# Retention, attention and a three-branch block: the order of the steps inside the attention groups, and where an output product starts

## The chip, the cores and the metric

The kernel runs on one core of a Trainium2 chip. The metric is the device time in microseconds (us) of one execution, as the median of several; lower is better. TensorE (PE) multiplies, ScalarE (ACT) and VectorE (DVE) do the element-wise work, SyncE (SP) issues most of the DMAs, GpSimd (POOL) is hardly used. Each engine runs its own list of instructions in order, and they meet through semaphores.

## The reference, cut to what matters

The input is one sequence of 256 tokens of width 2048, a context of 256 tokens and a memory of 256 tokens, all in float32. Two layers come first: a retention layer (8 heads) and an attention layer. Then comes a block with three attention branches. The change lies mostly in the attention layer:

```python
q = rms_norm(heads(h_lat @ w_in[q]), q_gain)      # 16 heads of 128
k = rms_norm(heads(h @ w_in[k]), k_gain)          # 4 kv heads; latent and context tokens
v = heads(h @ w_in[v]); g = h_lat @ w_in[g]
q, k = rope_2d(q), rope_2d(k)                     # latent tokens only
p = softmax(concat([q @ k_window, q @ k_ctx, sink]))   # each kv head serves a group of 4 q heads
y = (p @ v * silu(g)) @ w_out
x = x + gate * y
```

The retention layer ends likewise: `(norm(o) * silu(g)) @ w_out`, with `o` 512 wide for each of the 8 heads.

## The kernel before

**Weights.** All weight matrices come as one stream of 936 chunks of 128 x 1024 float32 (STREAM, built by `stream_order`). SP issues one DMA a chunk into one of four `raw` buffers, as soon as DVE is done with the chunk that was there (`sync_program`). A product is made of three in a reduced float32 format: the weights are split into `w_hi` (a copy by ACT, L921) and `w_lo` (the rest, a subtraction by DVE, L1429), the activations likewise into hi and lo, and PE adds hi*hi, hi*lo and lo*hi (`product`, L510 to L512). `w_hi` and `w_lo` have four buffers each too, so ACT may copy chunk n once PE is done with chunk n-4. On ACT and DVE `weights_to(c)` does all splits up to chunk c+3 that are not yet done; `ahead(what)` calls it with the last chunk of a tile. It is called at fixed places of the two programs, so a split waits for whatever stands ahead of it on its engine.

**Tiles and pairs.** `tile` (PE) makes 128 output columns of a product over all 16 k tiles: two chunks, 48 matmuls. `pair` makes 2 x 128 output columns over 4 k tiles (one chunk, 24 matmuls), for the output products: `attn_out(kv)` is 8 pairs, as is `ret_out(h)`. Its result is added to the residual `res` by DVE (`add_out`, L1608).

**Banks.** PSUM has eight banks, and `bank` takes them in turn. PE waits there until the bank's last result was read: `pair` takes both of its banks before its first matmul, a head's scores take two banks, its transposes two, a gate, a next q tile, a value product and `q_means` one each.

**Attention.** After the values (av), the four k tiles (ak) and the q tiles of group 0 (aq) are made. Each k tile is normed: a mean by PE (L708), a root by ACT (L959), a reciprocal, a scaling and a rotation by DVE (`norm`; the rotation waits until ACT has swapped halves of the tile, L992 and L993). Then four groups follow, one for each kv head. A step of a head is: `z` gate tile (PE), tanh (ACT, L986) and its product with the gate (DVE, L1497); `sc` scores (PE, L719), a masked read out of PSUM, maximum and so on (DVE, L1776 to L1788), exp (ACT, L1185), scaling to probabilities `a_s` (DVE, L1796); `tr` transposes (PE, L729), copied by ACT into `a_pt` (L1192); `pv` the value product (PE, L738), gated by DVE (L1803), whose hi part is a copy by ACT (`a_o_hi`, L1197) and whose lo part is DVE's (`a_o_lo`, L1806). The q tiles of the next group are made between them, their squares summed by `q_means` (L748), with a root by ACT and a reciprocal by DVE. The order of group kv on PE is

```
z0 z1 sc0 z2 sc1 tr0 z3 pv0 sc2 nq0 tr1 sc3 nq1 pv1 tr2 nq2 pv2 tr3 nq3 pv3 [o_lo(3)] attn_out(kv)
```

with nq the next group's q tiles (none in group 3) and `q_means` of the next group inside attn_out. ACT and DVE have lists in the same order. After group 3 DVE adds squares of the result (L1447), PE makes their mean x2 (L592), and the next block's input can be made (L1883).

## Time and profile before

| | us |
|---|---|
| median of three runs | 3464.83 |
| lowest and highest | 3459.5, 3465.22 |
| the profiled execution | 3462.32 |
| its span, first to last instruction | 3461.0 |
| PE busy in it | 3266.4 |
| DVE, ACT busy | 1710.4, 1260.8 |

The profile page gives each engine's busy time over the span and the chain of work that ended last. The trace behind it can be asked for the instructions of a stretch in order of time, for the waits of one engine, and for the busy time and the TensorE clock that was granted (1.00 is the full one) in any stretch. Times in the trace count from the span's start. Of the layers, retention ends at about 1863 us, the attention groups run from 2015 to 2368 us, and the last block takes the rest.

### The profile page before, as it was taken

The page shows a single profiled execution, that of the slowest core. Times are in us where ns is not written, and L with a number is a line of the kernel's source. Part 1 is how long each engine was busy: PE and PEld are TensorE (multiplying, and loading weights), DVE is VectorE, ACT ScalarE, POOL GpSimd, SP SyncE. Part 2 cuts the span into 40 slices and gives each one's busy share as a digit, 9 for nine tenths or more (in the row PEclk, how much of TensorE's full clock was granted, in tenths as well). Part 3 has the DMA queues.
Part 4 walks back from the last instruction along what each step waited for, and adds up shares of the span by engine and source line. Part 5 has one row for each costly group of instructions (what it writes and reads, how often), then busy time and mean ns, then how long its engine had stood idle before and what let it go on. Part 6 is the DMA issues. An engine that isn't in the chain of part 4 may idle for free.

```text
span 3461.0 us, 47818 instructions
## 1 busy us (share of the span) xinstructions
PE 3266.4 (94%) x20346; PEld 2791.9 (81%) x20346; DVE 1710.4 (49%) x2479; ACT 1260.8 (36%) x1785; POOL 0.2 (0%) x4
## 2 busy tenths in 40 slices
PE   6879999999999999999997989988999999999998
PEld 5657677777777777777766889987999999999998
DVE  5433343434333343443336566766665555555555
ACT  4342222222222222222224455544554444444443
POOL 0000000000000000000000000000000000000000
PEclk9989999999999999999998999999999999999999
DMA  7744423233332333333233234433445444455554
GB/s 304 289 187 158 179 107 110 104 128 122 110 128 95 113 109 128 122 110 128 86 142 138 86 122 146 138 131 137 162 149 168 149 158 161 156 190 199 193 188 153
DMA packets 141635, 508.93 MB, mean 147 GB/s; under 512 B 15344, under 2 KB 19568, under 8 KB 140656
## 3 DMA queue, kind: packets, MB, share of 16 engines
q1 hardware_dynamic: 137040, 493.03, 40.5%
q10 hardware_dynamic: 4384, 12.85, 1.0%
q8 instruction: 161, 2.64, 0.3%
q14 instruction: 50, 0.41, 0.0%
HBM read 501.62 MB, written 4.19 MB: 146 GB/s over the span
## 4 chain that ended last, share of the span: by engine, by line
PE 88%; DVE 4%; DMA 3%; ACT 3%; issue 2%; SPq 0%; ACTq 0%; DVEq 0%
PE bank L510 26%; PE bank L512 26%; PE bank L511 26%; DMA raw<-stream 3%; PE bank L563 2%; PE bank L653 2%; PE bank L719 1%; PE bank L738 1%; DVE w_lo L1429 1%; PE bank L639 1%; PE bank L655 1%; PE bank L729 1%; ACT a_s L1185 0%; ACT w_hi L921 0%; PE bank L579 0%
## 5 line engine op out<-in xcount | busy, mean ns | idle before, releaser
L510 PE MATMUL bank<-h_hi,w_hi 128*128 128x256 f32 (+1 forms) x4032 | 1268.1, 315 | 16.1 <-DVE w_lo L1429 13.8
L1429 DVE TENSOR_TENSOR w_lo<-raw,w_hi 128x1024 fp32r<-128x1024 f32 x744 | 901.4, 1223 | 757.4 <-ACT w_hi L921 753.3
L511 PE MATMUL bank<-h_lo,w_hi 128*128 128x256 f32 (+1 forms) x4032 | 1245.8, 309 | 0.0
L512 PE MATMUL bank<-h_hi,w_lo 128*128 128x256 f32 (+1 forms) x4032 | 1245.6, 309 | 0.0
L921 ACT ACTIVATE w_hi<-raw 128x1024 fp32r<-128x1024 f32 x744 | 780.3, 1057 | 1073.2 <-PE bank L512 608.1
L510 PEld LDWEIGHTS bank<-h_hi,w_hi 128*128 128x128 f32 x4032 | 762.5, 189 | 84.7 <-issue 34.0
L511 PEld LDWEIGHTS bank<-h_lo,w_hi 128*128 128x128 f32 x4032 | 764.0, 189 | 45.3 <-issue 3.3
L512 PEld LDWEIGHTS bank<-h_hi,w_lo 128*128 128x128 f32 x4032 | 762.0, 189 | 43.7
L510 PE MATMUL bank<-w_hi,h_hi 128*128 128x512 f32 x704 | 292.6, 416 | 47.8 <-DVE h_lo L1481 20.6
L511 PE MATMUL bank<-w_lo,h_hi 128*128 128x512 f32 x704 | 281.7, 400 | 0.0
L512 PE MATMUL bank<-w_hi,h_lo 128*128 128x512 f32 x704 | 281.4, 400 | 0.0
L1608 DVE SCALAR_TENSOR_TENSOR res<-bank,mod,res 128x256 f32<-128x256 f32 x320 | 134.2, 478 | 177.7 <-PE bank L512 177.6
L510 PE MATMUL bank<-o_hi,w_hi 128*128 128x512 f32 x512 | 201.2, 393 | 12.5 <-ACT vg L981 9.8
L510 PEld LDWEIGHTS bank<-w_hi,h_hi 128*128 128x128 f32 x704 | 136.7, 194 | 94.3 <-issue 40.2
L511 PE MATMUL bank<-o_lo,w_hi 128*128 128x512 f32 x512 | 200.2, 391 | 0.0
L512 PE MATMUL bank<-o_hi,w_lo 128*128 128x512 f32 x512 | 200.2, 391 | 0.0
L512 PEld LDWEIGHTS bank<-w_hi,h_lo 128*128 128x128 f32 x704 | 136.2, 193 | 30.7
L511 PEld LDWEIGHTS bank<-w_lo,h_hi 128*128 128x128 f32 x704 | 136.7, 194 | 29.6 <-issue 1.9
L563 PE MATMUL bank<-raw,cond 128*32 128x256 f32 x1536 | 115.7, 401 | 19.3 <-DMA raw<-stream 19.3
L510 PEld LDWEIGHTS bank<-o_hi,w_hi 128*128 128x128 f32 x512 | 96.7, 189 | 34.8 <-issue 15.0
L512 PEld LDWEIGHTS bank<-o_hi,w_lo 128*128 128x128 f32 x512 | 96.6, 189 | 20.3
L511 PEld LDWEIGHTS bank<-o_lo,w_hi 128*128 128x128 f32 x512 | 96.7, 189 | 19.8
(219 smaller groups left out, 2667.1 us busy)
## 6 DMA issues: line engine op xcount, KB each, us to landing
raw<-stream SPq DMA_DIRECT2D x936, 512.0 KB, 4.0
res<-tokens_in ACTq DMA_DIRECT2D x4, 1024.0 KB, 7.5
vg<-mem_in ACTq DMA_DIRECT2D x4, 512.0 KB, 8.9
res<-mem_kv ACTq DMA_DIRECT2D x2, 1024.0 KB, 9.4
out<-res SPq DMA_DIRECT2D x4, 512.0 KB, 3.0
mem_kv<-qk ACTq DMA_DIRECT2D x1, 1024.0 KB, 12.6
mem_kv<-vg ACTq DMA_DIRECT2D x1, 1024.0 KB, 15.8
tab<-tables ACTq DMA_DIRECT2D x1, 512.0 KB, 4.8
```

Of the source, the lines that this page charges most:

```text
L510: pe.matmul(out, sh, mh, start=start, stop=False)
L511: pe.matmul(out, sh, ml, start=False, stop=False)
L512: return pe.matmul(out, sl, mh, start=False, stop=stop)
L563: mm = pe.matmul(out[32 * j:32 * j + 32, 0:L], m.cond[:, 4 * c + j, :], m.raw[SLOT[chunk]][:, j * L:(j + 1) * L], start=c == 0, stop=c == 3)
L639: mm = pe.matmul(outs[mt][:, :], m.qk[:, 2 + dt, L + mt * P:L + (mt + 1) * P], m.qk[:, dt, :], start=dt == 0, stop=dt == 1)
L653: pe.matmul(out[:, :], m.v[:, 2 + mt, dv], m.s_ctx[:, mt, :], start=mt == 0, stop=mt == 1)
L655: mm = pe.matmul(out[:, LAT], m.v[:, mt, dv], m.s_lat[:, mt, :], start=False, stop=mt == 1, skip_group_check=True)
L719: mm = pe.matmul(out[:, at - a0:at - a0 + n], q[:, qs], k, start=i == 0, stop=i == len(pairs) - 1)
L729: mm = pe.transpose(out[:, at:at + P], probs[:, qt, kt * P:(kt + 1) * P], ident)
L921: act.activation(m.w_hi[n % SLOTS][:, :], m.raw[SLOT[raw]][:, :], ACT.Copy).then_inc(s.hi, 1)
L1429: dve.tensor_tensor(m.w_lo[slot][:, :], m.raw[SLOT[raw]][:, :], m.w_hi[slot][:, :].bitcast(F32), ALU.subtract).then_inc(s.lo, 1)
L1608: i = dve.scalar_tensor_tensor(out=m.res[:, tile, cols], in0=psum(*what)[:, cols], scalar=m.mod[layer][:, 2 * KT + tile, side:side + 1], i ...
```

## The change

1. `pair` can be given four semaphore values (`ready`), one for each k tile. Then it loops k outside and output j inside, and waits for tile k's value ahead of its products. The first pair of every `ret_out` and `attn_out` uses it, in place of one wait for `o_lo` of the last tile ahead of the product.
2. The k norms on ACT and DVE call `weights_to` between the root or scaling and the swap or rotation.
3. Gate tile 0 of the next group and `q_means` of the next group are made at the end of a group, ahead of `attn_out`; the groups 1 to 3 begin with z1.
4. `attn_out(2)` moves into group 3, behind sc1. On ACT and DVE its pairs 0 to 2 stand ahead of sc(1), the other five behind it.
5. In group 3, z2 and z3 stand behind sc2 and sc3.

The stream of chunks is put into the same order. Per group and engine no instruction is added or taken away.

```diff
@@ -182,14 +182,26 @@
         tile(("ak", i), "attn_w_in", q_w + i * P)
     for h in range(GROUP):
         tile(("aq", 0, h), "attn_w_in", h * P)
-    for i in range(ATTN_KV):
-        for h in range(GROUP):
+
+    def az(i, *heads):
+        for h in heads:
             tile(("az", i, h), "attn_w_in", q_w + 2 * kv_w + (GROUP * i + h) * P)
-        if i < ATTN_KV - 1:
-            for h in range(GROUP):
-                tile(("aq", i + 1, h), "attn_w_in", (GROUP * (i + 1) + h) * P)
+
+    def attn_out(i):
         for n in range(KT // 2):
             out.append((("attn_out", i), "attn_w_out", 0, 4 * i, 4, n * 2 * P, 2 * P))
+    az(0, 0)
+    for i in range(ATTN_KV - 1):
+        az(i, 1, 2, 3)
+        for h in range(GROUP):
+            tile(("aq", i + 1, h), "attn_w_in", (GROUP * (i + 1) + h) * P)
+        az(i + 1, 0)
+        if i < ATTN_KV - 2:
+            attn_out(i)
+    az(ATTN_KV - 1, 1)
+    attn_out(ATTN_KV - 2)
+    az(ATTN_KV - 1, 2, 3)
+    attn_out(ATTN_KV - 1)
     for n in range(2):
         for c in range(8):
             values(("bv", n), "w_in_2", 2 * W_A + n * 512, c)
@@ -525,16 +537,17 @@
                              k == 0, k == k_tiles - 1)
             mm.then_inc(s.mm, 1)
 
-    def pair(what, c, cols, acts, k0=0):
+    def pair(what, c, cols, acts, k0=0, ready=None):
 
         xh, xl = acts
         outs = [bank(*what, j) for j in range(2)]
         wh, wl = weights(c)
-        for j in range(2):
-            for k in range(4):
-                w = slice(k * 2 * P + j * P, k * 2 * P + (j + 1) * P)
-                mm = product(outs[j][:, 0:cols.stop - cols.start], (wh[:, w], wl[:, w]),
-                             (xh[:, k0 + k, cols], xl[:, k0 + k, cols]), k == 0, k == 3)
+        for j, k in [(j, k) for k in range(4) for j in range(2)] if ready else [(j, k) for j in range(2) for k in range(4)]:
+            if ready and j == 0:
+                pe.wait_ge(*ready[k])
+            w = slice(k * 2 * P + j * P, k * 2 * P + (j + 1) * P)
+            mm = product(outs[j][:, 0:cols.stop - cols.start], (wh[:, w], wl[:, w]),
+                         (xh[:, k0 + k, cols], xl[:, k0 + k, cols]), k == 0, k == 3)
         mm.then_inc(s.mm, 1)
 
     def values_banks(what, tiles):
@@ -686,9 +699,9 @@
             beside(h, "end")
             ada(1, 21)
             ada_turn(1, 20)
-        pe.wait_ge(*s["o_lo"].at(h, 3))
         for n in range(KT // 2):
-            pair(("ret_out", h, n), FIRST["ret_out", h] + n, BOTH, (m.o_hi, m.o_lo))
+            pair(("ret_out", h, n), FIRST["ret_out", h] + n, BOTH, (m.o_hi, m.o_lo),
+                 ready=[s["o_lo"].at(h, k) for k in range(4)] if n == 0 else None)
     ada_turn(1, 21)
     ada(1, 22)
     mean("x1", BOTH)
@@ -775,36 +788,57 @@
         def next_q(h):
             if not last:
                 tile(("aq", kv + 1, h), LAT)
-        z(0)
+        def attn_out(kv):
+            for n in range(KT // 2):
+                pair(("attn_out", kv, n), FIRST["attn_out", kv] + n, LAT, (m.a_o_hi, m.a_o_lo),
+                     ready=[s["o_lo"].at("a", kv, k) for k in range(4)] if n == 0 else None)
         if kv == 0:
+            z(0)
             q_means(0)
         z(1)
         pe.wait_ge(*s["roped"].at("aq", kv, 1))
         pe.wait_ge(*s["roped"].at("ak", ATTN_KV - 1))
         sc(0)
-        z(2)
-        sc(1)
-        tr(0)
-        z(3)
-        pe.wait_ge(*s["v_set"].at("a", kv))
-        pv(0)
-        sc(2)
-        next_q(0)
-        tr(1)
-        sc(3)
-        next_q(1)
-        pv(1)
-        tr(2)
-        next_q(2)
-        pv(2)
-        tr(3)
-        next_q(3)
-        pv(3)
-        pe.wait_ge(*s["o_lo"].at("a", kv, 3))
-        for n in range(KT // 2):
-            if n == 2 and not last:
-                q_means(kv + 1)
-            pair(("attn_out", kv, n), FIRST["attn_out", kv] + n, LAT, (m.a_o_hi, m.a_o_lo))
+        if not last:
+            z(2)
+            sc(1)
+            tr(0)
+            z(3)
+            pe.wait_ge(*s["v_set"].at("a", kv))
+            pv(0)
+            sc(2)
+            next_q(0)
+            tr(1)
+            sc(3)
+            next_q(1)
+            pv(1)
+            tr(2)
+            next_q(2)
+            pv(2)
+            tr(3)
+            next_q(3)
+            pv(3)
+            tile(("az", kv + 1, 0), LAT)
+            q_means(kv + 1)
+            if kv < ATTN_KV - 2:
+                attn_out(kv)
+        else:
+            sc(1)
+            attn_out(kv - 1)
+            tr(0)
+            pe.wait_ge(*s["v_set"].at("a", kv))
+            pv(0)
+            sc(2)
+            z(2)
+            tr(1)
+            pv(1)
+            sc(3)
+            z(3)
+            tr(2)
+            pv(2)
+            tr(3)
+            pv(3)
+            attn_out(kv)
     mean("x2", LAT)
 
 
@@ -1148,11 +1182,12 @@
         act.wait_ge(*source)
         act.activation(m.nsq[i][:, :], x, ACT.Square).then_inc(*s["squared"].up(*what))
 
-    def norm(what, i, x, before):
+    def norm(what, i, x, before, after):
 
         if before:
             act.wait_ge(*s["roped"].at(*before))
         root(("norm", *what), s["n_meaned"].at(*what), m.nrstd[i][:, :])
+        weights_to(FIRST[after])
         n = x.shape[1]
         swap(what, m.nrstd[i][:, 0:n * L].rearrange("p (a b) -> p a b", b=L), x, 32, s["n_scaled"].at(*what))
 
@@ -1201,11 +1236,12 @@
     for n in range(1, ATTN_KV):
         ahead(("ak", n))
         norm_squares(("ak", n), n % 2, m.a_k[:, n, :], banks.at("ak", n))
-        norm(("ak", n - 1), (n - 1) % 2, m.a_k[:, n - 1:n, LAT], ("ak", n - 3) if n >= 3 else None)
+        norm(("ak", n - 1), (n - 1) % 2, m.a_k[:, n - 1:n, LAT], ("ak", n - 3) if n >= 3 else None,
+             ("ak", n + 1) if n < ATTN_KV - 1 else ("aq", 0, 0))
     ahead(("aq", 0, 0))
     q_square(0, 0)
     n = ATTN_KV - 1
-    norm(("ak", n), n % 2, m.a_k[:, n:n + 1, LAT], ("ak", n - 2))
+    norm(("ak", n), n % 2, m.a_k[:, n:n + 1, LAT], ("ak", n - 2), ("aq", 0, 1))
     ahead(("aq", 0, 1))
     q_square(0, 1)
     q_swap(0, 0, ("ak", 2))
@@ -1240,39 +1276,60 @@
         def next_swap(n):
             if not last:
                 q_swap(kv + 1, n, ("aq", kv, n))
-        z(0)
+        def attn_out(kv, *pairs):
+            for n in pairs:
+                weights_to(FIRST["attn_out", kv] + n)
+                if kv == ATTN_KV - 1:
+                    for j in range(2):
+                        k = 2 * n + j
+                        act.wait_ge(*banks.at("attn_out", kv, n, j))
+                        square("x2", k, (sq_out(k, LAT), m.res[:, k, LAT]))
         if kv == 0:
+            z(0)
             q_root(0)
         z(1)
         sc(0)
-        z(2)
-        sc(1)
-        tr(0)
-        z(3)
-        pv(0)
-        sc(2)
-        next_q(0)
-        tr(1)
-        sc(3)
-        next_q(1)
-        pv(1)
-        tr(2)
-        next_swap(0)
-        next_q(2)
-        pv(2)
-        tr(3)
-        next_q(3)
-        pv(3)
-        next_swap(1)
-        for n in range(KT // 2):
-            weights_to(FIRST["attn_out", kv] + n)
-            if n == 2 and not last:
-                q_root(kv + 1)
-            if last:
-                for j in range(2):
-                    k = 2 * n + j
-                    act.wait_ge(*banks.at("attn_out", kv, n, j))
-                    square("x2", k, (sq_out(k, LAT), m.res[:, k, LAT]))
+        if not last:
+            z(2)
+            sc(1)
+            tr(0)
+            z(3)
+            pv(0)
+            sc(2)
+            next_q(0)
+            tr(1)
+            sc(3)
+            next_q(1)
+            pv(1)
+            tr(2)
+            next_swap(0)
+            next_q(2)
+            pv(2)
+            tr(3)
+            next_q(3)
+            pv(3)
+            next_swap(1)
+            tanh(("az", kv + 1, 0), m.a_g[:, 0, :])
+            q_root(kv + 1)
+            if kv < ATTN_KV - 2:
+                attn_out(kv, *range(8))
+        else:
+            attn_out(kv - 1, 0, 1, 2)
+            sc(1)
+            attn_out(kv - 1, 3, 4, 5, 6, 7)
+            tr(0)
+            pv(0)
+            sc(2)
+            z(2)
+            tr(1)
+            pv(1)
+            sc(3)
+            z(3)
+            tr(2)
+            pv(2)
+            tr(3)
+            pv(3)
+            attn_out(kv, *range(8))
     root(("mean", "x2"), s["meaned"].at("x2"), m.rstd[:, LAT])
 
 
@@ -1730,13 +1787,14 @@
         done(what)
         dve.tensor_copy(x, psum(*what)[:, 0:cols.stop - cols.start]).then_inc(*banks.up(*what))
 
-    def norm(what, i, x, latent, gain):
+    def norm(what, i, x, latent, gain, after):
 
         dve.wait_ge(*banks.at("norm", *what))
         dve.reciprocal(m.nrstd[i][:, :], m.nrstd[i][:, :]).then_inc(*s["n_rstd"].up(*what))
         dve.wait_ge(*s["n_rstd"].at(*what))
         dve.scalar_tensor_tensor(out=x, in0=x, scalar=gain, in1=m.nrstd[i][:, :], op0=ALU.mult, op1=ALU.mult
                                  ).then_inc(*s["n_scaled"].up(*what))
+        weights_to(FIRST[after])
         n = latent.shape[1]
         cos, sin = [m.rope1[:, j, :].unsqueeze(1).broadcast_to([P, n, L]) for j in range(2)]
         rotate(what, latent, m.nrstd[i][:, 0:n * L].rearrange("p (a b) -> p a b", b=L), cos, sin, s["n_scaled"].at(*what))
@@ -1757,8 +1815,8 @@
         dve.wait_ge(*banks.at("q_mean", kv))
         dve.reciprocal(m.q_rstd[:, :, :], m.q_rstd[:, :, :]).then_inc(*s["q_rstd"].up(kv))
 
-    def k_norm(n):
-        norm(("ak", n), n % 2, m.a_k[:, n, :], m.a_k[:, n:n + 1, LAT], m.gains[:, 1:2])
+    def k_norm(n, after):
+        norm(("ak", n), n % 2, m.a_k[:, n, :], m.a_k[:, n:n + 1, LAT], m.gains[:, 1:2], after)
 
     def softmax(what, x, width, numbers, mask, sink, rstd=None):
 
@@ -1808,9 +1866,9 @@
     tile_in(("ak", 0), m.a_k[:, 0, :], BOTH)
     for n in range(1, ATTN_KV):
         tile_in(("ak", n), m.a_k[:, n, :], BOTH)
-        k_norm(n - 1)
+        k_norm(n - 1, ("ak", n + 1) if n < ATTN_KV - 1 else ("aq", 0, 0))
     q_in(0, 0)
-    k_norm(ATTN_KV - 1)
+    k_norm(ATTN_KV - 1, ("aq", 0, 1))
     q_in(0, 1)
     q_rotate(0, 0)
     q_in(0, 2)
@@ -1836,39 +1894,54 @@
             if not last:
                 q_in(kv + 1, h)
 
-        z(0)
+        def attn_out(kv, *pairs):
+            for n in pairs:
+                weights_to(FIRST["attn_out", kv] + n)
+                dve.wait_ge(s.mm, FIRST["attn_out", kv] + n + 1)
+                for j in range(2):
+                    add_out(("attn_out", kv, n, j), 2 * n + j, (0,), 1)
+                if kv == ATTN_KV - 1:
+                    for j in range(2):
+                        add_square("x2", 2 * n + j, LAT)
         if kv == 0:
+            z(0)
             q_reciprocal(0)
         z(1)
         dve.wait_ge(*s["q_rstd"].at(kv))
         sc(0)
-        z(2)
-        sc(1)
-        z(3)
-        pv(0)
-        sc(2)
-        next_q(0)
-        sc(3)
-        next_q(1)
-        pv(1)
         if not last:
+            z(2)
+            sc(1)
+            z(3)
+            pv(0)
+            sc(2)
+            next_q(0)
+            sc(3)
+            next_q(1)
+            pv(1)
             q_rotate(kv + 1, 0)
-        next_q(2)
-        pv(2)
-        next_q(3)
-        pv(3)
-        if not last:
+            next_q(2)
+            pv(2)
+            next_q(3)
+            pv(3)
             q_rotate(kv + 1, 1)
-        for n in range(KT // 2):
-            weights_to(FIRST["attn_out", kv] + n)
-            dve.wait_ge(s.mm, FIRST["attn_out", kv] + n + 1)
-            for j in range(2):
-                add_out(("attn_out", kv, n, j), 2 * n + j, (0,), 1)
-            if n == 2 and not last:
-                q_reciprocal(kv + 1)
-            if last:
-                for j in range(2):
-                    add_square("x2", 2 * n + j, LAT)
+            silu(("az", kv + 1, 0), m.a_g[:, 0, :])
+            q_reciprocal(kv + 1)
+            if kv < ATTN_KV - 2:
+                attn_out(kv, *range(8))
+        else:
+            attn_out(kv - 1, 0, 1, 2)
+            sc(1)
+            attn_out(kv - 1, 3, 4, 5, 6, 7)
+            pv(0)
+            sc(2)
+            z(2)
+            pv(1)
+            sc(3)
+            z(3)
+            pv(2)
+            pv(3)
+            attn_out(kv, *range(8))
     reciprocal(("mean", "x2"), m.rstd[:, LAT], ("x2",))
 
 
```

## Rows read from the trace of the kernel before

**Rows 1.** The page: the span, and one engine's busy time, share and instructions.

```profile
span 3461.0 us, 47818 instructions
PE 3266.4 (94%) x20346; PEld 2791.9 (81%) x20346; DVE 1710.4 (49%) x2479; ACT 1260.8 (36%) x1785; POOL 0.2 (0%) x4
```

**Rows 2.** PE's waits, 1950 to 2430 us: releaser, us in total, times, longest.

```profile
PE bank L510 <- DVE a_o_lo L1806: 8.6, 4, 3.0
PE bank L738 <- ACT a_pt L1192: 8.5, 3, 4.4
PE bank L592 <- DVE sq_sum L1447: 7.2, 1, 7.2
PE bank L510 <- DVE w_lo L1429: 5.6, 2, 5.1
...
PE bank L738 <- issue: 3.8, 4, 1.9
```

**Rows 3.** PE's waits, 250 to 1820 us (the retention heads).

```profile
PE bank L510 <- ACT vg L981: 9.8, 7, 1.5
...
PE bank L510 <- DVE w_lo L1429: 2.7, 1, 2.7
```

**Rows 4.** Stretches on PE: us, busy (instructions), granted clock, DMA share, GB/s.

```profile
2109.20:2120.50 11.30, 11.30 (x98) 1.00 0.54 186
2182.40:2199.40 17.00, 17.00 (x145) 1.00 0.57 196
```

**Rows 5.** Timeline of PE: start, us, instruction, idle before it and releaser.

```profile
2003.83 0.58 PE L510 MATMUL bank<-h_hi,w_hi 128*128 128x256 f32 x1 [5.15 <-DVE w_lo L1429]
...
2265.09 0.38 PE L510 MATMUL bank<-a_o_hi,w_hi 128*128 128x256 f32 x1 [2.98 <-DVE a_o_lo L1806]
...
2346.34 0.38 PE L510 MATMUL bank<-a_o_hi,w_hi 128*128 128x256 f32 x1 [1.42 <-DVE a_o_lo L1806]
```

**Rows 6.** Timeline of DVE in the last k norms and behind them.

```profile
1990.55 0.43 DVE L1488 TENSOR_TENSOR a_k<-a_k,a_rope 128x256 f32<-128x256 f32 x1 [1.83 <-ACT a_rstd L993]
...
2001.43 0.43 DVE L1488 TENSOR_TENSOR a_k<-a_k,a_rope 128x256 f32<-128x256 f32 x1 [1.82 <-ACT a_rstd L993]
...
2010.34 2.35 DVE L1429 TENSOR_TENSOR w_lo<-raw,w_hi 128x1024 fp32r<-128x1024 f32 x2
```

**Rows 7.** Timeline of PE: `q_means`, then a value product, scores and transposes.

```profile
2180.66 1.84 PE L748 MATMUL bank<-a_ones,a_sq 128*128 128x1 f32 x16
...
2318.36 1.97 PE L738 MATMUL bank<-a_pt,a_v 128*128 128x256 f32 x8 [0.64 <-issue]
2320.16 1.88 PE L719 MATMUL bank<-a_k,a_q 128*128 128x512 f32 x4
2321.87 1.04 PE L729 MATMUL bank<-tab,a_s 128*128 128x128 f32 x8
```

**Rows 8.** Timeline of DVE, groups 2 and 3.

```profile
2269.20 1.22 DVE L1429 TENSOR_TENSOR w_lo<-raw,w_hi 128x1024 fp32r<-128x1024 f32 x1
...
2303.47 1.53 DVE L1776 SCALAR_TENSOR_TENSOR a_s<-bank,a_q_rstd,a_mask 128x512 f32<-128x512 f32 x2
...
2309.76 2.35 DVE L1429 TENSOR_TENSOR w_lo<-raw,w_hi 128x1024 fp32r<-128x1024 f32 x2
...
2349.38 0.88 DVE L1608 SCALAR_TENSOR_TENSOR res<-bank,mod,res 128x256 f32<-128x256 f32 x2 [1.35 <-PE bank L512]
```

**Rows 9.** Timeline of ACT, group 3.

```profile
2295.18 1.28 ACT L986 ACT_TABLE_LOAD   x1
...
2317.20 1.05 ACT L1192 ACTIVATE a_pt<-bank 128x512 f32<-128x512 f32 x2
```

**Rows 10.** Stretches on PE behind a wait, columns as in rows 4.

```profile
2003.80:2009.60 5.80, 5.77 (x27) 0.50 0.50 184
2265.10:2267.50 2.40, 2.40 (x13) 0.63 0.67 218
2329.00:2340.90 11.90, 8.88 (x25) 0.65 0.00 0
```

## Prediction

> **What bounds the kernel now.** Read the page's busy shares first: TensorE (PE) is busy 94% of 3461.0 us, VectorE (DVE) 49% [rows 1]. So only what PE stands still for, or runs slowly for, can be won. I then listed PE's waits over the attention part alone, 1950 to 2430 us, where nearly the whole diff acts: 8.6 us for a_o_lo in four waits (one ahead of each group's output product), 8.5 us for a_pt in three (all in group 3), 7.2 us for the last square sum, 5.6 us for w_lo in two (while the q tiles of group 0 are made), 3.8 us marked "issue" ahead of value products [rows 2]. That is 34 us, besides what the slower clock costs behind the longer gaps. Group 3 is the weak place: it has no next q tiles to lay between its heads.
>
> **Output products begin with the k tiles that are there.** Twelve first pairs (8 ret_out, 4 attn_out) get four waits in place of one, and their 24 products go k outside, j inside. In the heads PE's waits at these places are for ACT's copies of the values out of PSUM (L981: 9.8 us, seven times), which free the banks that the pair takes before its first product, and once 2.7 us for w_lo, the pair's own weights [rows 3]. Neither goes: both must be there before k tile 0 too. Gain in ret_out: 0. The extra waits are on semaphores long raised; a boundary between two attn_out pairs, which has three such waits, doesn't show in a stretch of 145 product rows that took 17.00 us (0.117 each) [rows 4]. Cost taken: 0; at the most 0.1 us at each of 36, 3.6 us.
>
> **Weights inside the k norms.** Before, PE waited 5.15 us at 2003.83 for the second half of aq2's weights, since DVE copied none between its two norms [rows 5]. DVE stood 1.83 and 1.82 us in these norms until ACT's swap was done [rows 6]. The change puts one w_lo (1.15 of a row of two at 2.35) into each of these holes, so DVE's own chain moves up by about 1.13 us twice, 2.3 us. PE's chain: aq1 without its 0.47 us wait; aq2's second half at about 1998 (2003.83 less 5.15 and 0.47), w_lo there at 1999.7 (2001.43 less the hole of 1.82, less 1.13, plus 1.2): 2 us of waiting left; aq3's first half to 2005.5; its second needs the row that began at 2010.34 [rows 6], now 2008.1 plus 1.15, so PE waits 3.8 us there, where before its late and slow start had hidden that. The stall mostly moves. What counts is DVE's chain into the first softmax, since PE waited behind it too (the longest "issue" wait, 1.9 us, is at group 0's first pv) [rows 2]. It comes 2.3 us earlier; the clock behind the 3.8 us gap may make PE the late one by some 0.6. Taken: 1.7 us. Bounds: 0.4, if PE runs slowly through aq3 and z0, and 2.3; 8.2 if all the 5.6 us of waiting and the slow clock behind it went (27 product rows in 5.80 us [rows 10], 2.6 more than at 0.117), which the 2010.34 row speaks against.
>
> **Groups 0 and 1.** The next group's gate tile 0 (5.65 us: 98 rows in 11.30 us are two tiles) [rows 4] and q_means (1.7 us) [rows 7] now stand between pv(3) and attn_out. o_lo is ready at most 3.0 us behind pv(3), so their two waits go (8.6 less 2.98 and 1.42: 4.2 us [rows 2, 5]), and some 0.2 of slow restart: 4.4 us. What is late next? The pair's weights: ACT copies ao1 and ao2 after its swap, DVE's w_lo follow its rotation, which ends 7.1 us behind pv(3) (2269.20 against 2262.1) [rows 5, 8]: ao1 there at +8.3, needed at +10.2; ao2 at +9.5, needed at +13.0; ao3 after the gate and reciprocal at +11.4, needed at +15.9. No new wait. With one gate tile less ahead of sc(0), the weights split by then are the same chunks as before, and the table loads on ACT are as many. SP's queue keeps its order with the stream, and a DMA is issued as soon as w_lo of four chunks before is done, so it doesn't decide. Taken: 4.4; if the tile covered nothing, 0.
>
> **From the end of group 2 to x2's mean.** Let u be the end of pv(3) of group 2, 2262.1 (2265.09 less the wait of 2.98) [rows 5]. Before, pv(3) of group 3 ended at 2344.9 (2346.34 less 1.42) [rows 5], u+82.8. Now PE: gate 0 to u+5.65, q_means 7.35, gate 1 13.0, sc(0) and sc(1) at 1.71 each 16.4 [rows 7], then attn_out(2) at 2.83 a pair: pair 2 ends at 24.9. Pair 3 takes the banks of sc(1) (eight banks in turn: az, q_mean, z1, four scores, p0 to p2 lie between). DVE frees them only in sc(1), which stands behind three pairs. DVE: free at 7.1, two w_lo, silu, reciprocal, sinks to 9.85; ACT two w_hi (1.0 each) to 12.05, a table load of 1.28 and tanh to 13.75 [rows 9]; DVE silu 14.2, softmax 0 at 6.3 (2303.47 to 2309.76) 20.5, three steps of w_lo 1.22 and two adds 0.88 to 26.8, the score reads (1.4 of the row of 1.53) 28.2 [rows 8]. **PE waits about 3.4 us ahead of pair 3: a new wait.** Five pairs then to 42.5. In the heads' steps ACT now has exp, two w_hi (2.0) and tanh ahead of its a_pt copies (1.05) [rows 9], so each pv waits: tr(0) 43.4, gap 1.0; pv 1.8, sc 1.7, z2 5.65, tr 0.9 to 54.3, gap 1.95; the same with z3 to 66.2, gap 1.9; pv, tr 68.8, gap 1.3; pv(3) ends at 73.8. Gain 9.0 us. Behind the 2.98 us wait the granted clock was 0.63 over the first 2.4 us, and 13 product rows were done in it where 20 go at 0.117 [rows 10]; the next ones are slow in part too. I charge 1.5 us for the 3.4 us gap. Left 7.5.
> The tail is DVE's: PE waits 7.20 us for the square sum. Of the 1.42 us o_lo wait that "k tiles that are there" removes (three k tiles are 2.1 us of work, o_lo(3) comes after 1.4), DVE gets what it waited for PE in its first step, 1.35 [rows 8]: I count 1.3. 8.8 us in all. Bounds: 3, if the new gaps are twice as long (9.6 us more at most, less what PE has in hand), and 13, if pair 3 finds its banks free and the clock stays high.
>
> **Sum:** 1.7 + 4.4 + 8.8 = 14.9 us off the profiled execution's 3462.3, 3447.4. That execution is 2.5 us below the median of the three, 3464.83; on it the same gain gives 3449.9. I say 3449.
>
> **Rivals.** (A) The queue on DVE is worse than worked out: sc(1), its exp and the weights ao6 and ao7 come one behind the other, PE waits at pair 6 too, and group 3 keeps its length. For: DVE has 6.3 us a softmax and PE 2.83 us a pair. Against: ao6's w_lo ends at 34.4, PE needs it at 36.8. Then only 1.7 + 4.4 and some 2 of the rest are won: 3455 to 3458.
> (B) Slower: the clock. The gap at pair 3 drops the granted clock and the four gaps of 1 to 2 us hold it down to the end of group 3. From 2329.0 to 2340.9, between gaps of 4.41 and 2.98 us, the mean was 0.65, against 0.50 when wholly low [rows 10]. At the low level a product has 0.213 us in place of 0.117: five pairs of 24 cost 11.5 more, z2 and z3 (96) 9.5, the rest 4; 25 us against 16 won: 3471 to 3474. It decides if the low clock lasts over 170 products. Against: behind the 5.15 us wait it had risen again after 27 products [rows 5, 10].
> The Trainium skill ("TensorE: Matmul & The Clock Gate", section "A second HAM failure mode: psum-queue depth-cycling") says that short idles between groups of products, from cycling through PSUM banks, can make the clock swing and take throughput though each product looks fast. That is this rival. The trace agrees in part: 0.65 in the stretch of bursts between gaps [rows 10], 1.00 in the two gapless ones [rows 4]; no row has gaps of 1 to 2 us between tiles of 5.7 us.
> (C) More is won: the q tiles' stall goes whole (8.2 for 1.7), or the banks are free at pair 3 (3.4 and 1.5): 3440 to 3445.
> (D) It doesn't do what it says: the gate tile hides o_lo, but PE then waits as long for DVE, which has the same work: 3461 to 3465.
>
> **Chances.** Forecast 0.64 (its own range 3444 to 3455), A 0.16, B 0.05, C 0.10, D 0.05. Range 3440 to 3460: B, D and part of A lie outside, and as much again may be wrong in my queue order. 0.2% is 6.9 us, what a measurement here can tell from none: under 3457.9 is faster. Forecast, C and more than half of A: 0.84 faster; the rest of A and D 0.11; slower 0.05.
>
> **What would show it.** Right: no PE wait on a_o_lo longer than 0.2 us; a gap of 3 to 4 us inside attn_out(2) on a bank that DVE's L1776 frees; a wait for w_lo of about 4 us still ahead of aq3's second half; a_pt waits of 1 to 2 us, four times; the square-sum wait 7 us or more. Wrong: no gap in attn_out(2) (C), a clock under 0.9 over group 3 (B), or a last group as long as the 82.8 us (A, D).

## The result, and the profile after

The changed kernel took 3440.96 us, the median of four runs (3433.42 to 3442.48), beside 3462.16 of the kernel before (four runs, 3458.78 to 3465.22). The ratio is 0.9935, 95% interval [0.9916, 0.9954]. So it takes 0.65% less time; it is faster, as forecast, and by more: I had said 3449. The profiled execution took 3442.48.

The page, as in [rows 1]: span, and busy time of PE.

```profile
span 3441.2 us, 47818 instructions
PE 3263.2 (95%) x20346; PEld 2789.0 (81%) x20346; DVE 1709.3 (50%) x2479; ACT 1260.3 (37%) x1785; POOL 0.2 (0%) x4
```

The instructions are as many and the busy times the same within 4 us. Of the 19.8 us that the span lost, 3.2 are busy time of PE, and through the other 16.6 it had stood still. PE's waits over the attention part (1950 to 2420 us), columns as in [rows 2]:

```profile
PE bank L605 <- DVE sq_sum L1504: 7.4, 1, 7.4
PE bank L522 <- DVE w_lo L1486: 5.3, 2, 3.6
PE bank L522 <- DVE h_lo L1956: 4.4, 1, 4.4
PE bank L751 <- issue: 4.0, 4, 1.9
PE bank L751 <- ACT a_pt L1227: 3.8, 3, 1.4
PE bank L522 <- DVE a_s L1834: 2.9, 1, 2.9
```

Against [rows 2]: the 8.6 us on a_o_lo (lo part of the attention output) are gone, the 8.5 on a_pt became 3.8, w_lo still costs 5.3, and 2.9 us on DVE's read of the scores are new. The single places on PE, answering to [rows 5], with the ends of the stretch in which I measure below:

```profile
1956.30 0.59 PE L721 MATMUL bank<-a_sq,a_ones 128*128 128x512 f32 x1
...
1997.66 0.39 PE L522 MATMUL bank<-h_hi,w_hi 128*128 128x256 f32 x1 [1.74 <-DVE w_lo L1486]
...
2007.36 0.39 PE L522 MATMUL bank<-h_hi,w_hi 128*128 128x256 f32 x1 [3.58 <-DVE w_lo L1486]
...
2279.77 0.36 PE L522 MATMUL bank<-a_o_hi,w_hi 128*128 128x256 f32 x1 [2.92 <-DVE a_s L1834]
...
2295.30 0.45 PE L751 MATMUL bank<-a_pt,a_v 128*128 128x256 f32 x1 [0.79 <-issue]
...
2306.67 0.70 PE L751 MATMUL bank<-a_pt,a_v 128*128 128x256 f32 x2 [1.35 <-ACT a_pt L1227]
...
2353.22 1.19 PE L605 MATMUL bank<-sq_sum,ones_mean 128*128 128x256 f32 x2 [7.45 <-DVE sq_sum L1504]
```

The 5.15 us stall has become 1.74 and 3.58. DVE at the new wait:

```profile
2271.71 0.89 DVE L1854 TENSOR_SCALAR a_s<-a_s,a_numbers 128x512 f32<-128x512 f32 x2
2272.51 1.22 DVE L1486 TENSOR_TENSOR w_lo<-raw,w_hi 128x1024 fp32r<-128x1024 f32 x1
2273.65 0.87 DVE L1665 SCALAR_TENSOR_TENSOR res<-bank,mod,res 128x256 f32<-128x256 f32 x2
...
2277.49 0.86 DVE L1665 SCALAR_TENSOR_TENSOR res<-bank,mod,res 128x256 f32<-128x256 f32 x2
2278.27 1.39 DVE L1834 SCALAR_TENSOR_TENSOR a_s<-bank,a_q_rstd,a_mask 128x512 f32<-128x512 f32 x2
```

The rows show the queue: the scores of head 1 lay in their banks long before, but DVE reads them only behind three steps of weights and adds, at 2278.27, and PE's pair 3 begins 0.11 us after that read ends.

I measure in the stretch from the first k norm's mean product on PE (before at 1958.31) to x2's mean product (before at 2375.59): all edits but the pairs of ret_out lie in it. What lies outside it took 3034 to 3054 us in the 14 traces, in no order that follows the edits, so gains of a few us can't be read from whole spans. Each kernel was traced twice (the second traces are two of the experiments, e12 and e13). The table cuts the stretch at the starts of the last value product pv(3) of groups 0, 2 and 3:

| us | before, twice | after, twice | gain of the means | forecast |
|---|---|---|---|---|
| norm to pv(3), group 0 | 123.21, 121.93 | 121.36, 119.65 | 2.1 | 1.7 |
| to pv(3), group 2 | 178.60, 181.32 | 172.77, 172.01 | 7.6 | 4.4 |
| to pv(3), group 3 | 82.80, 82.79 | 71.57, 73.36 | 10.3 | 7.5 |
| to x2's mean | 32.67, 32.66 | 31.22, 31.22 | 1.4 | 1.3 |
| whole stretch | 417.28, 418.70 | 396.92, 396.24 | 21.4 | 14.9 |

### The profile page after: what moved, and what is told of

It reads as the page before. It is cut to its first block, busy times and chain, and to the rows that moved or that the text cites. A ratio compares the mean times of both kernels' runs of the same rounds, so it can differ in the third digit from the quotient of the medians.

```text
span 3441.2 us, 47818 instructions
## 1 busy us (share of the span) xinstructions
PE 3263.2 (95%) x20346; PEld 2789.0 (81%) x20346; DVE 1709.3 (50%) x2479; ACT 1260.3 (37%) x1785; POOL 0.2 (0%) x4
## 4 chain that ended last, share of the span: by engine, by line
PE 88%; DVE 4%; DMA 3%; ACT 3%; issue 2%; SPq 0%; ACTq 0%; DVEq 0%
PE bank L522 26%; PE bank L524 26%; PE bank L523 25%; DMA raw<-stream 3%; PE bank L576 2%; PE bank L666 2%; PE bank L751 2%; PE bank L732 1%; PE bank L652 1%; DVE w_lo L1486 1%; PE bank L668 1%; PE bank L742 1%; ACT w_hi L955 1%; PE bank L592 0%; PE bank L657 0%
## 5 line engine op out<-in xcount | busy, mean ns | idle before, releaser
L522 PE MATMUL bank<-h_hi,w_hi 128*128 128x256 f32 (+1 forms) x4032 | 1268.8, 315 | 16.6 <-DVE w_lo L1486 14.2
## 6 DMA issues: line engine op xcount, KB each, us to landing
mem_kv<-qk ACTq DMA_DIRECT2D x1, 1024.0 KB, 12.7
```

The costliest lines, as they stand in the source:

```text
L522: pe.matmul(out, sh, mh, start=start, stop=False)
```

## The experiments

"Stretch" is the one of the table, in one trace of each. Ratios are to the kernel before, with 95% intervals. The four sections of the stretch in every trace (us), and how long the eight products of group 0's first value product took in it (1.97 at full clock, more where the clock had fallen):

| | to pv(3), group 0 | group 2 | group 3 | x2's mean | stretch | first pv |
|---|---|---|---|---|---|---|
| before | 123.21 | 178.60 | 82.80 | 32.67 | 417.28 | 3.00 |
| before again (e13) | 121.93 | 181.32 | 82.79 | 32.66 | 418.70 | 1.97 |
| e1: k tile order only | 121.59 | 176.11 | 79.55 | 31.21 | 408.46 | 1.97 |
| e2: norms only | 120.97 | 178.47 | 82.59 | 32.66 | 414.68 | 2.85 |
| e3: groups' order only | 121.61 | 172.97 | 71.67 | 32.65 | 398.90 | 1.97 |
| after | 121.36 | 172.77 | 71.57 | 31.22 | 396.92 | 3.41 |
| after again (e12) | 119.65 | 172.01 | 73.36 | 31.22 | 396.24 | 1.97 |
| e5: after, less k tile order | 120.96 | 172.61 | 72.34 | 32.74 | 398.65 | 3.27 |
| e8: after, attn_out(2), z2 and z3 put back | 120.97 | 172.63 | 77.55 | 31.23 | 402.39 | 2.97 |
| e10: after, attn_out(2) put back | 120.96 | 173.16 | 78.88 | 31.21 | 404.22 | 3.42 |
| e4: after, sc(1) behind pair 2 | 119.68 | 173.17 | 69.43 | 31.21 | 393.48 | 1.97 |
| e6: e4, tr(1) and tr(2) ahead of the gates | 120.97 | 172.80 | 68.40 | 32.62 | 394.79 | 3.34 |
| e9: e6, three splits out of the tail | 119.30 | 174.12 | 68.08 | 28.29 | 389.77 | 1.97 |
| e11: e4, three splits out of the tail | 120.97 | 172.37 | 69.41 | 26.71 | 389.47 | 3.50 |

The first section is 1.3 to 2.1 us longer where that value product was slow, in kernels that are alike up to there. In the old order the wait for o_lo takes this back: attn_out(0) (in e1 its last k tile) got o_lo 126.56 us behind the first k norm's mean in before, e13 and e1 alike. In the new order nothing does, so two stretches can differ by that much without any edit, and an edit is better read in the sections where it acts.

**One part of the change at a time.** e1 is the kernel before with the k tile order only:

```diff
...
-        for j in range(2):
-            for k in range(4):
+        for j, k in [(j, k) for k in range(4) for j in range(2)] if ready else ...:
+            if ready and j == 0:
+                pe.wait_ge(*ready[k])
...
```

> The kernel before with the first part of the change alone: the first pair of each output product waits for the k tiles one by one. Theory A (the gaps add up): ret_out unchanged; in groups 0 to 2 the waits for a_o_lo of 1.5, 2.7 and 3.0 us shrink by the 2.1 us that three k tiles last, to nothing, 0.6 and 0.9; with gaps that short the slow clock behind the third (1.5 us) goes too; in group 3 only 1.35 us, since DVE's additions set the end. Together 5.5 to 8.5 us less than before. Rival B (what stands behind is late anyway: the fourth pair's weights, copied by DVE behind its rotation): 1 to 2 us. Two traces of the same code differ by some 2 us elsewhere.

Measured: 3450.91 us, 0.9968 [0.9947, 0.999]; stretch 408.46, 8.8 less than 417.28.

```profile
PE bank L739 <- ACT a_pt L1193: 9.1, 3, 4.4
...
PE bank L510 <- DVE a_o_lo L1807: 2.6, 3, 0.9
```

Three o_lo waits of 0.86 to 0.92 are left of 1.46, 2.74 and 2.98, group 3's 1.42 is gone, and so are the slow products behind the 2.98. Alone, this small edit is worth 8.8 us, just over theory A's range. (Up to 0.6 of it is chance: PE came early to attn_out(0), since group 0's first value product ran at full pace here, and could do 2.1 us of products ahead of the wait, where the first trace of before had 1.46 us of waiting to fill.)

e2 is the kernel before with the norms' edit only, on ACT and DVE:

```diff
         root(("norm", *what), ...)
+        weights_to(FIRST[after])
         swap(what, ...)
```

> The kernel before with the second part alone: weights split inside the k norms. Theory A: DVE's chain into group 0's first softmax comes 2.3 us earlier and PE follows it: 1.9 to 2.3 us less, with PE waits for w_lo of about 1.7 and 3.6 us left in the q tiles. Rival B: the whole wait of 5.6 us and the slow clock behind it go: 8 us less. Rival C: nothing, since PE waits as long further on.

Measured: 3459.14, 0.9996 [0.9976, 1.0017]; stretch 414.68, 2.6 less. DVE's chain is 2.2 us earlier, as forecast: o_lo is there for attn_out(0) 124.34 us behind the first k norm's mean in place of 126.56. The stall is 1.73 and 3.49 us in place of 5.15: the w_lo were moved up, and the next ones are late, as theory A has it.

e3 is the changed kernel without both of these (the groups' new order only):

```diff
-        weights_to(FIRST[after])
...
-            if ready and j == 0:
-                pe.wait_ge(*ready[k])
...
+            pe.wait_ge(*s["o_lo"].at("a", kv, 3))
```

> The changed kernel with the one wait for o_lo and without the splits inside the norms: only the order of the steps in the groups is changed. Theory A (additive): the changed kernel's gain less 2.1 us (norms) and 1.4 us (tail of group 3), so 15 to 18 us less than before, 3.5 us more than the changed kernel. Rival B (the order works only with the k tiles waits, because attn_out(2) and the others would stall on o_lo): under 12 us less than before.

Measured: 3447.82, 0.9958 [0.9937, 0.9979]; stretch 398.90, 18.4 less, a little more than theory A's range. But 1.6 of it lie in the first section, where nothing is changed, and in the new order no wait takes them back; 16.8 are left for the order. The order carries most. Its o_lo waits in groups 0 to 2 are gone without the k tile order: both edits hide the same wait, so their gains don't add up (8.8 and 18.4 and 2.6 against 20.4).

e5 takes only the k tile order out of the changed kernel (the diff of e1, undone):

```diff
...
-                pe.wait_ge(*ready[k])
...
+            pe.wait_ge(*s["o_lo"].at("a", kv, 3))
...
```

> The changed kernel with one wait for the last k tile ahead of each first pair, as before. Theory A (only the last attn_out finds o_lo late, since the gate tile covers it in the others): the stretch is 396.9 plus 1.0 to 1.4, 398.3, with one a_o_lo wait of 1.42 in group 3 and none in groups 0 to 2; the median 0.5 to 2 us above the changed kernel's. Theory B (the k tile order costs in the eleven other places what it gains in this one): the stretch longer by 1.4 but the whole span no longer than the changed kernel's.

Measured: 3442.34, 0.9936 [0.9917, 0.9956]; stretch 398.65, so 1.7 and 2.4 above the two traces with it, and one wait of 1.43 us for a_o_lo, ahead of attn_out(3). Theory A holds, with 1.5 in the last section (32.74 against 31.22) in place of 1.0 to 1.4. Every trace with the k tile order and the old tail has 31.21 to 31.23 there but e6 (its last value product was slow), and every one without it 32.65 to 32.74. On the whole kernel the difference is too small to tell. Of ret_out no trace shows a gain or a cost: the nine traces with the k tile order reach the first k norm's mean at 1951.6 to 1958.0 us, the five without it at 1952.1 to 1962.1.

**Inside group 3.** e8 puts attn_out(2), z2 and z3 back in their old places (PE's part; ACT's and DVE's lists likewise):

```diff
...
-            if kv < ATTN_KV - 2:
-                attn_out(kv)
+            attn_out(kv)
         else:
+            z(2)
             sc(1)
-            attn_out(kv - 1)
             tr(0)
+            z(3)
...
```

> The changed kernel, but attn_out(2) stays at the end of group 2, and z2 and z3 of group 3 stay where they were: of the order only gate tile 0 and q_means ahead of attn_out is left, besides the norms and the k tiles waits. Theory A (additive): from the last k norm's mean to x2's mean 417.3 us before, less 2.3 (norms), 7.2 (the waits for a_o_lo of groups 0 to 2), 1.5 (slow clock behind the third) and 1.4 (tail): 405 us; the gaps of 4.4 and 3 us for a_pt and their slow clock stay in group 3. The changed kernel has 396.9 there. Rival B: the gate tile is all that matters, and group 3 is DVE's chain whatever PE does: within 2 us of the changed kernel, 398 us.

Measured: 3441.89, 0.9939 [0.992, 0.9958]; stretch 402.39, between the theories and nearer to A. The a_pt waits of group 3 are back:

```profile
PE bank L748 <- ACT a_pt L1222: 7.9, 3, 4.4
```

e10 is e8 with z2 and z3 behind sc2 and sc3:

```diff
-            z(2)
             sc(1)
             tr(0)
-            z(3)
...
             pv(0)
             sc(2)
+            z(2)
             tr(1)
+            pv(1)
             sc(3)
-            pv(1)
+            z(3)
...
```

> As the kernel with only gate 0 moved, and z2 and z3 of group 3 also behind sc(2) and sc(3), but attn_out(2) still at the end of group 2. Theory A (the output product is what fills the first softmax; the gates alone only move the gap): PE stands some 5 to 6 us ahead of tr(0) instead, the a_pt waits shrink to 1 to 1.4 us, and the stretch stays within 2 us of 405. Rival B (the gates do it): 5 us less, about 400.

Measured: 3444.15, 0.9939 [0.9918, 0.9961]; stretch 404.22. Without an output product between sc(1) and tr(0), the gates' new place only moves the holes forward, 3.97 us ahead of tr(0) and 4.55 behind it, while the a_pt waits shrink to 1.06 to 1.35, as theory A has it:

```profile
2290.51 0.44 PE L739 MATMUL bank<-tab,a_s 128*128 128x128 f32 x2 [3.97 <-DVE a_s L1846]
...
2296.36 0.77 PE L748 MATMUL bank<-a_pt,a_v 128*128 128x256 f32 x1 [4.55 <-issue]
```

So it is attn_out(2)'s place that fills group 3: from 78.88 in the third section to 71.57 and 73.36, 7.3 and 5.5 us.

e4 removes the new wait. On PE sc(1) comes behind pair 2, so that its banks are asked for later and pair 3 takes others:

```diff
+            attn_out(kv - 1, 0, 1, 2)
             sc(1)
-            attn_out(kv - 1)
+            attn_out(kv - 1, 3, 4, 5, 6, 7)
```

> The changed kernel, with sc(1) of group 3 behind pair 2 of attn_out(2) on PE too, as it stands on DVE and ACT already. Theory A (pair 3 waits for the two banks that sc(1)'s scores hold until DVE comes to them behind the three pairs): the 2.92 us gap ahead of pair 3 is gone, since pair 3 then takes the banks of pair 0, and the kernel is 2.5 to 3 us faster than the changed one. Rival B (pair 3 waits because DVE's softmax is in front of its weights): the gap stays or moves to pair 6 or tr(0), same time within 1 us.

Measured: 3438.4, 0.9932 [0.9912, 0.9953]; stretch 393.48, 3.4 and 2.8 below the changed kernel's. In the third section, where the edit acts, it is 2.1 below the first trace, which is the 2.92 us wait less the 0.77 of a short one for weights that comes later, and 3.9 below the second, which had slow products behind the wait. Theory A holds:

```profile
2285.04 0.36 PE L522 MATMUL bank<-a_o_hi,w_hi 128*128 128x256 f32 x1 [0.77 <-DVE w_lo L1487]
```

e6 adds to e4 that tr(1) and tr(2) stand ahead of z2 and z3, on PE and ACT:

```diff
-            z(2)
             tr(1)
+            z(2)
```

> The kernel with sc(1) behind pair 2, and in group 3 tr(1) and tr(2) also ahead of z2 and z3, on PE and ACT, so that ACT's copies into a_pt lie behind a gate tile of 5.7 us. Theory A (the a_pt waits of 1.35 us are the copy behind the transposes, nothing longer): both waits go, 2.7 us less than with sc(1) alone, 390.8 against 393.5 from the last k norm's mean to x2's mean. Rival B (the softmax chain on DVE and ACT is as long, so PE waits further on, at tr(2), tr(3) or pv): under 1 us less.

Measured: 3435.76, 0.9921 [0.9892, 0.995]; stretch 394.79, 1.3 longer than e4's, as much as the first section (its first value product was slow); the last two together are 0.4 longer. The two waits of 1.35 are gone, but the last one of group 3 grew from 1.06, and the value product behind it was slow (3.19 us in place of 1.99):

```profile
2320.14 0.70 PE L751 MATMUL bank<-a_pt,a_v 128*128 128x256 f32 x2 [2.56 <-ACT a_pt L1228]
```

Theory A fails, rival B holds: PE meets the wait at the last head. That ACT and DVE have the same work for a head is the likely reason; no run takes work from them there.

**The tail.** e9 is e6 without the splits of the next block's weights in the last three pairs of attn_out(3), on ACT and DVE; one of them follows behind the squares, the others in the next block:

```diff
-                weights_to(FIRST["attn_out", kv] + n)
+                if kv < ATTN_KV - 1 or n < 5:
+                    weights_to(FIRST["attn_out", kv] + n)
...
+    weights_to(FIRST["bv", 0], 1)
```

> The same, and in attn_out(3) the splits of the next block's weights (steps 5 to 7, one w_hi and one w_lo each) are left out of DVE's and ACT's last steps; one is made while the mean is on its way, the others in the next block's loop. Theory A (the 6.6 to 7.4 us wait ahead of x2's mean is DVE's: 8 steps of 3.45 us against 2.83 of PE): the wait falls by 4 to 5 us, and as many are won over the version without this. Rival B (the splits only move: the next block's first chunks then wait for w_lo): the mean comes 4 to 5 us earlier, but PE waits 3 to 4 us more behind it, and under 1.5 us is won.

Measured: 3432.57, 0.991 [0.9879, 0.994]; stretch 389.77, 5.0 less than e6, 4.3 of it in the last section. e11 is the same edit on e4:

> The changed kernel with two edits only: sc(1) of group 3 behind the third pair of attn_out(2), and no splits of the next block's weights on DVE and ACT in the last three pairs of attn_out(3). The transposes stay where the change has them. Theory A (effects add up): the stretch from the first k norm's mean product to x2's mean product is 393.5 less the 5.0 that the tail's edit gave with the transposes moved, 388.5 us, and the median 3430 to 3434, since later weights take 2 us of it back. Theory B (the transposes' move was what let the tail gain): 391 to 393.5 and a median near 3437.

Measured: 3433.28, 0.9915 [0.9897, 0.9932]; stretch 389.47, 4.0 less than e4, and 4.5 in the last section, near theory A's 5.0. PE's waits in it:

```profile
PE bank L522 <- DVE w_lo L1489: 6.0, 3, 3.5
PE bank L522 <- DVE h_lo L1961: 5.8, 3, 5.2
...
PE bank L605 <- DVE sq_sum L1507: 2.1, 1, 2.1
```

In e4 DVE has a w_lo in each of these steps (1.23 us, with 0.39 of waiting for ACT's copy), two adds (0.87) and two square sums (0.95), 3.45 us a step, where PE needs 2.83 a pair:

```profile
2340.22 1.23 DVE L1487 TENSOR_TENSOR w_lo<-raw,w_hi 128x1024 fp32r<-128x1024 f32 x1 [0.39 <-ACT w_hi L956]
...
2342.32 0.95 DVE L1505 TENSOR_TENSOR sq_sum<-sq_sum,sq 128x256 f32<-128x256 f32 x2
2343.67 1.22 DVE L1487 TENSOR_TENSOR w_lo<-raw,w_hi 128x1024 fp32r<-128x1024 f32 x1 [0.39 <-ACT w_hi L956]
```

The square sum's wait goes from 6.6 in e4 to 2.1; 1.4 us of it comes back as later waits for h_lo (5.8 against 4.4). e9 and e11 are the fastest versions, some 8 us below the changed kernel by their medians and 7 by the stretch. The intervals of their ratios overlap the changed kernel's, so on the whole kernel this is likely and not shown; in the stretch it is. They can't be told from each other, so the transposes' place is worth nothing that these runs show.

**What repeats.** The changed kernel again (e12), and the kernel before again (e13), both without an edit:

> The changed kernel once more, unchanged, to see what repeats. Theory A (the gap of 2.9 us ahead of pair 3 doesn't bring the granted clock down): the same gap within 0.05, and the five pairs behind it again in 13.9 us. Theory B (whether it falls is chance): the gap the same, the five pairs 15 us or more. The stretch from the first k norm's mean product to x2's mean product 396.9 within 1; more than 1 apart would be the pace of products (113.5 or 117.8 ns) falling another way.

Measured: 3441.32, 0.995 [0.9925, 0.9975]; stretch 396.24. The ratio was 0.9935 the first time: the same kernel repeats to 0.15%. The gap was 2.61, since PE came 0.3 us later with its three pairs, so it was not the same within 0.05; the five pairs behind it took 15.41 us, as theory B has it. The first 5 us behind the gap, in the first trace and in the second (us, busy and instructions, granted clock, DMA share, GB/s):

```profile
2279.70:2284.70 5.00, 4.93 (x43) 1.00 0.21 75
```

```profile
2275.60:2280.60 5.00, 4.93 (x30) 0.67 0.25 91
```

> The kernel before once more, unchanged, for its scatter: the stretch 417.3 within 1.5, the waits of 2.98 us behind pv(3) of group 2 and of 4.41 us in group 3 the same within 0.1. Theory A: the slow products behind the 2.98 wait return (11 us or more over what gapless products take, as before). Theory B: the clock behind that wait falls by chance, and a trace in which it doesn't is 2 to 3 us shorter there.

Measured: one execution of 3473.85, used for its trace only; stretch 418.70. Of the 11.5 us that its span is longer than the first trace's, 10 lie outside the stretch. Of its three o_lo waits of 2.75, 2.98 and 2.98 us, the first and the third have slow products behind them (7.35 and 7.33 us for the first two pairs, 48 products, in place of 5.73), the second not. First 4 us behind the second, the third and the first:

```profile
2170.20:2174.20 4.00, 3.95 (x34) 1.00 0.36 135
2260.20:2264.20 4.00, 3.92 (x20) 0.58 0.44 138
2078.60:2082.60 4.00, 3.98 (x24) 0.67 0.39 134
```

Theory A holds for group 2's wait (slow in both traces of the kernel before and in e2), but group 0's, fast in the first trace at 1.46 us, was slow here. That wait is itself 1.3 us longer than in the first trace, since PE came to it 1.3 us earlier and o_lo no sooner.

## Why the prediction was right in kind and short in size

**The failed step is the term "From the end of group 2 to x2's mean"**: 8.8 us forecast, 12.7 in the changed kernel's first trace (82.80 less 71.57, and 1.45) and 11.8 over both. The waits were where I had put them, but they were shorter, and I had charged for a slow clock that mostly didn't come. The term stayed within its own bounds, 3 to 13. Its parts, each as the prediction put it:

- "About 3.4 us ahead of pair 3: a new wait": there, at that pair, on that read; 2.92 and 2.61. PE came there at 24.5 behind the end of group 2 (forecast 24.9), DVE's read ended at 27.3 (28.2). 0.5 us of the error.
- "Each pv waits", 1.0, 1.95, 1.9 and 1.3, together 6.15: there, four times, 0.79, 1.35, 1.34 and 1.07, together 4.55. 1.6 us of the error. A step came out at 11.37 us (2295.30 to 2306.67), where I had summed 12.0.
- "I charge 1.5 us for the 3.4 us gap": nothing in the first trace (120 products in 13.87 us), 1.5 in the second. In e3 and e5, with gaps of 2.65 and 2.62 at that place, nothing either (granted clock 1.00 behind them, 13.86 and 14.37 us). One of four; as a certainty the charge was too high, its size was right.
- The tail, 1.3: 1.45.

In the working "pv, tr 68.8" should be 70.8; the end at 73.8 and the gain of 9.0 are worked out rightly.

**Groups 0 and 1.** The mechanism held: no o_lo wait is left there, and no other took its place. Forecast 4.4; 5.8 between the first traces, 7.6 over both. Of the 1.4 over in the first traces, 1.15 is pace: attn_out(0) and attn_out(1) took 22.93 and 23.12 us before (5.73 and 17.20; 5.92 and 17.20) and 22.04 and 22.86 after. In the second trace of before the waits were longer and one had slow products behind it: what is taken away is itself not the same in each execution. Over both traces this term is short by 3.2 us, as much as the failed one (3.0); I had given it no bound above 4.4.

**The norms.** 1.7 forecast, 1.85 between the first traces, 2.1 over both, and 2.2 in e2 by DVE's chain. Between traces alike in the first value product (121.93 and 119.65, both at full pace) it is 2.3, the 2.3 by which I had DVE's chain move up. "The stall mostly moves", to 2 and 3.8: it did, to 1.74 and 3.58.

**The k tile order.** Forecast at no gain in ret_out and 1.3 at the tail; e5 gives 1.5 in the tail. What I didn't say is that without the groups' order it is worth 8.8.

**The sum.** The stretch gave 20.4 where I had 14.9, 5.5 us; and the median of before that I put it on, 3464.83, was 2.7 above that of four runs, 3462.16. Together 8.2, against the 8.0 between 3449 and 3440.96. The time fell 1 us inside my range: the range held by luck as much as by working.

**The rivals.** A (group 3 keeps its length) is refuted by 82.8 against 71.6 and 73.4. B (the clock stays low over group 3): from the end of group 2 to the last scores' and value products of group 3 (2252.40 to 2320.10 us) the granted clock was 1.00 in the first trace, and over the same part of the second (2250.00 to 2321.40) 0.98, where it fell behind the gap at pair 3 and rose again within the five pairs. The section "A second HAM failure mode: psum-queue depth-cycling" of the Trainium skill's page "TensorE: Matmul & The Clock Gate" says that short idles between groups of products can make the clock swing. For gaps as short as these the traces don't agree: four gaps of 0.8 to 1.35 us between gate tiles, scores and transposes cost their own length, and the products behind them ran at full pace, in both traces of the changed kernel. The shortest gap in the stretch with slow work behind it is the one of 1.90 or 1.91 us ahead of group 0's first value product: slow in 8 of the 11 traces that have it (3.41 us in place of 1.97 in the changed kernel's first), and in none of the three where it is 1.70 or 1.71. C (banks free at pair 3, or the q tiles' stall gone) didn't happen, yet the time fell where I had put C, for the reasons above; e4 made its first half happen and gained 2.1 and 3.9 us more in the third section. D (PE waits as long for DVE) is refuted by the stretch, 396.9 against 417.3.

## What to carry to other kernels

Two edits that hide the same wait don't add up: measure each on the kernel before and on the kernel after, and keep the cheaper. When an output product is put into a stage where the vector engines are the bound, look at who frees the banks that its pairs take, and put the stage's own products behind the pairs that don't need them; then look for work of the next stage that stands in the bound engine's last steps. A gap removed is worth its length, and sometimes the slow products behind it; a forecast should carry that part as a chance, not as a sum.

## What the runs showed that I had not expected

**Two paces at full clock.** The same 192 products of an attn_out take 22.04 or 22.86 us, with nothing between, at a granted clock of 1.00. In the changed kernel's first trace, attn_out(0) and attn_out(1) (columns as above):

```profile
2087.00:2108.60 21.60, 21.60 (x192) 1.00 0.68 217
2172.70:2195.10 22.40, 22.40 (x192) 1.00 0.68 209
```

That is 0.113 and 0.117 us a product, the slower no busier with transfers. In the new order it falls differently from execution to execution (attn_out(0) and attn_out(1) are slow and fast in e3, both fast in e11 and e12, both slow in e9), and within the attention part it changes only at an instruction of another kind. Over 240 products it makes 1 us. It isn't quite free of the edits: in the four traces with the old order (before, e13, e1, e2) the six pairs of attn_out(0) to attn_out(2) behind q_means took 17.20 or 17.21 us, the slower pace, in all 12 places, while in the ten with the new order attn_out(0) and attn_out(1) were slow in 9 of 20. So a part of the gain in groups 0 and 1 may be pace that the order changes; the cause is open.

**The clock behind equal gaps.** Behind waits of 2.6 to 3.0 us the granted clock over the first 4 or 5 us fell to 0.58 to 0.67 in some places and executions and stayed 1.00 in others (four traces of the bank gap, 2.61 to 2.92: one fell; three of the 2.98 us wait ahead of attn_out(2): all fell; two of 2.98 ahead of attn_out(1): none). Even the longer gap of 3.48 to 3.58 us ahead of aq3's second half left the clock at 1.00 in two traces of ten (e2 and e8). What decides is open.
